# Joining the two products of each scan part on GpSimd ahead of the state-space read-out

## What is computed

```python
def combine(e1, e2):
    a1r, a1i, b1r, b1i = e1
    a2r, a2i, b2r, b2i = e2
    return (a2r * a1r - a2i * a1i, a2r * a1i + a2i * a1r,
            a2r * b1r - a2i * b1i + b2r, a2r * b1i + a2i * b1r + b2i)

_, _, xr, xi = lax.associative_scan(combine, (a_re, a_im, x_re0, x_im0), axis=1)
y = (jnp.einsum('bsgp,ghp->bsgh', xr, c_re.astype(f32))
     - jnp.einsum('bsgp,ghp->bsgh', xi, c_im.astype(f32))
     + d_skip.astype(f32).reshape(SSM_GROUPS, SSM_GROUP) * ug)
y = jax.nn.gelu(y.reshape(bsz, s, SSM_WIDTH)).astype(u.dtype)
```

## Time and profile before

| | us |
|---|---|
| median of three runs | 3403.2 |
| lowest and highest of them | 3398.81 and 3407.45 |
| span of the profiled execution | 3397.2 |
| TensorE busy in it | 3362.4 |
| VectorE busy | 2500.3 |
| ScalarE busy | 1963.3 |
| GpSimd busy | 736.1 |

### The profile page before, as it was taken

The page is one execution under the profiler, slowest core; times in us unless marked ns, Lnnn a source line. Parts: engine busy times, 40 slices in busy tenths (PEclk is TensorE's granted clock), DMA queues, the critical chain, the costliest instruction groups (busy, mean ns, idle before and its releaser), DMA issues.

```text
span 3397.2 us, 80038 instructions
## 1 busy us (share of the span) xinstructions
PE 3362.4 (99%) x29184; PEld 3319.9 (98%) x29184; DVE 2500.3 (74%) x4438; ACT 1963.3 (58%) x3483; POOL 736.1 (22%) x709
## 2 busy tenths in 40 slices
PE   8999999999999999999999999999999999999999
PEld 7999999999999999999999998999999999999999
DVE  7886688788875555676788879998667776666555
ACT  5456655677765555555555556765565665555554
POOL 1001130377777723555000000000000000000000
PEclk9999999999999999999999999999999999999999
DMA  8867788577777766877898864545555555555555
GB/s 325 335 221 253 248 299 303 161 187 190 186 193 194 194 204 225 271 244 249 320 341 338 335 218 132 176 160 183 162 189 192 187 190 192 192 191 196 187 192 179
DMA packets 234085, 758.61 MB, mean 223 GB/s; under 512 B 60072, under 2 KB 63664, under 8 KB 221104
## 3 DMA queue, kind: packets, MB, share of 16 engines
q1 hardware_dynamic: 167328, 608.57, 52.8%
q0 software_dynamic: 62624, 139.63, 15.0%
q10 hardware_dynamic: 3952, 7.91, 0.7%
HBM read 732.78 MB, written 21.11 MB: 222 GB/s over the span
## 4 chain that ended last, share of the span: by engine, by line
PE 94%; DVE 4%; ACT 1%; issue 1%; DMA 1%; DVEq 0%; SPq 0%; ACTq 0%
PE PS L502 24%; PE PS L508 23%; PE PS L507 23%; PE PS L651 7%; PE PS L661 7%; PE PS L659 7%; DVE wlo L1701 1%; DVE big L1695 0%; PE PS L934 0%; DMA raw<-peer_v_dram 0%; PE PS L761 0%; DVE big L1628 0%; PE PS L923 0%; PE PS L880 0%; PE PS L946 0%
## 5 line engine op out<-in xcount | busy, mean ns | idle before, releaser
L1061 ACT ACTIVATE whi<-raw 128x512 fp32r<-128x512 f32 x1864 | 1157.8, 630 | 1022.8 <-PE PS L508 652.3
L1557 DVE TENSOR_TENSOR wlo<-raw,whi 128x512 fp32r<-128x512 f32 x1480 | 1024.9, 706 | 605.9 <-ACT whi L1061 585.6
L502 PE MATMUL PS<-tok_parts_hi,whi 128*128 128x256 f32 x2048 | 569.4, 278 | 0.8 <-ACT big L1286 0.7
L508 PE MATMUL PS<-tok_parts_hi,wlo 128*128 128x256 f32 x2048 | 568.3, 277 | 0.0
L651 PE MATMUL PS<-whi,ev_parts_hi 128*128 128x256 f32 x2032 | 561.8, 276 | 1.1 <-DVE wlo L1557 1.1
L661 PE MATMUL PS<-whi,ev_parts_lo 128*128 128x256 f32 x2032 | 562.1, 277 | 0.0
L507 PE MATMUL PS<-tok_parts_lo,whi 128*128 128x256 f32 x2030 | 561.7, 277 | 0.0
L659 PE MATMUL PS<-wlo,ev_parts_hi 128*128 128x256 f32 x2026 | 559.9, 276 | 0.0
L1701 DVE TENSOR_TENSOR wlo<-raw,whi 128x512 fp32r<-128x512 f32 x564 | 381.6, 695 | 129.2 <-ACT whi L1150 84.1
L434 POOL DMA_INDIRECT gates_dram<-big x256 | 427.0, 1668 | 200.2 <-issue 91.1
L1150 ACT ACTIVATE whi<-raw 128x512 fp32r<-128x512 f32 x436 | 271.4, 629 | 250.4 <-PE PS L508 247.5
(11 more groups left out here) (552 smaller groups left out, 8201.3 us busy)
## 6 DMA issues: line engine op xcount, KB each, us to landing
raw<-peer_u_dram SPq DMA_DIRECT2D x256, 512.0 KB
raw<-peer_v_dram SPq DMA_DIRECT2D x256, 512.0 KB
raw<-w_in_dram SPq DMA_DIRECT2D x240, 512.0 KB
big<-w_mod_dram POOLq DMA_DIRECT2D x96, 1024.0 KB, 6.6
raw<-w_up_dram SPq DMA_DIRECT2D x176, 512.0 KB
raw<-w_down_dram SPq DMA_DIRECT2D x88, 512.0 KB
raw<-w_out_dram SPq DMA_DIRECT2D x64, 512.0 KB
gates_dram<-late POOLq DMA_DIRECT2D x16, 1024.0 KB, 9.0
```

Source lines behind the costliest of these rows:

```text
L502: pe.matmul(out, hi, rhi, start=start, stop=False, **more)
L508: return pe.matmul(out, lo, rhi, start=False, stop=stop, **more)
L1061: f(whi[:, m % PAIRS, quarter(q)], raw[:, m % RING, quarter(q)], ACT.Copy).then_inc(hi_ready, 1)
L1557: dv.tensor_tensor(wlo[:, m % PAIRS, quarter(q)], raw[:, m % RING, quarter(q)], whi[:, m % PAIRS, quarter(q)], ALU.subtract).then_inc(lo_r ...
```

## The change

GpSimd gets two adds for each part, `join(n)`: `ta = ta - tb` when VectorE has finished `tb` (new semaphore `s5_real`), and `p = p + q_` when it has finished `p` (`s5_x`). The read-out then takes two terms, `ta` with `cc[0]` and `p` with `cc[1]`, eight matmuls in place of sixteen, waits for the joins (`s5_joined`), and stands one chunk later (`k == 1`). The negated block of coefficients is no longer made. VectorE waits for `tb` as before, by the new semaphore. The list `RESET` stays.

```diff
--- before.py
+++ after.py
@@ -324,6 +324,7 @@
         lam_in, lam_a, lam_b, lam_c = (sem("l_" + n) for n in "in a b c".split())
         bc_in = [sem(f"s5_bcin{s}") for s in range(2)]
         c_in = sem("s5_cin")
+        s5_real, s5_joined = sem("s5_real"), sem("s5_joined")
         bc_used, s5_lam, s5_raw, s5_bu, s5_angr, s5_sinr, s5_x, s5_y, s5_ys, s5_gel = (
             sem("s5_" + n) for n in "bcused lam raw bu ang sin x y ys gelu".split())
         up_pre, up_silu, act_ready = (sem("up_" + n) for n in "pre silu ready".split())
@@ -473,12 +474,24 @@
                     pool.wait_ge(modw_used, part * KC + kc + 1)
                     pool.dma_start(modring_late[:, kc % MOD_RING, :],
                                    d["w_mod"][part * KC + kc]).then_inc(modw_in[kc % MOD_RING], 16)
+            def join(n):
+
+                p, q_, ta, tb = s5_set[n % 2]
+                pool.wait_ge(s5_real, n + 1)
+                pool.tensor_tensor(ta, ta, tb, ALU.subtract).then_inc(s5_joined, 1)
+                pool.wait_ge(s5_x, n + 1)
+                pool.tensor_tensor(p, p, q_, ALU.add).then_inc(s5_joined, 1)
+
             pool.wait_ge(stage_lo, N_SUB)
             pool.dma_start(cst[:, :, :, :], d["s5_c"]).then_inc(c_in, 16)
             for n in range(8):
                 if n >= 2:
                     pool.wait_ge(bc_used, n - 1)
                 pool.dma_start(bst[:, n % 2, :, :], d["s5_b"][n]).then_inc(bc_in[n % 2], 16)
+                if n >= 2:
+                    join(n - 2)
+            join(6)
+            join(7)
             for r in range(HEADS):
                 pool.wait_ge(qk_ready, 16 + r + 1)
                 if r == 0:
@@ -926,13 +939,13 @@
 
             def read_out(n):
 
-                p, q_, ta, tb = s5_set[n % 2]
-                pe.wait_ge(s5_x, n + 1)
+                p, _, ta, _ = s5_set[n % 2]
+                pe.wait_ge(s5_joined, 2 * n + 2)
                 pe.wait_ge(s5_ys, n)
-                for k, (part, of) in enumerate(((0, ta), (2, tb), (1, q_), (1, p))):
+                for part, of in enumerate((ta, p)):
                     for q in range(4):
                         last = pe.matmul(PS[32 * q:32 * q + 32, 6, 0:SEQ], cc[:, part, 4 * n + q, :], of[:, q, :],
-                                         start=k == 0, stop=k == 3)
+                                         start=part == 0, stop=part == 1)
                 last.then_inc(s5_y, 1)
 
             def spread_two(r):
@@ -988,7 +1001,7 @@
                 if c == 1:
                     mod_turn(3, 7)
                 n, k = divmod(c - SCAN, 5)
-                if k == 0 and 1 <= n <= 8:
+                if k == 1 and 1 <= n <= 8:
                     read_out(n - 1)
                 if k == 3 and -1 <= n < 7:
                     project(n + 1)
@@ -2059,7 +2072,6 @@
                 elif c == 2:
                     link(dv.tensor_tensor(ct[:, 1, :, :], ci, across(cre), ALU.mult))
                 elif c == 3:
-                    dv.tensor_tensor(cc[:, 2, :, :], ct[:, 0, :, :], cc[:, 0, :, :], ALU.subtract)
                     dv.tensor_tensor(cc[:, 0, :, :], cc[:, 0, :, :], ct[:, 0, :, :], ALU.subtract)
                 else:
                     link(dv.scalar_tensor_tensor(cc[:, 1, :, :], cc[:, 1, :, :], -1.0, ct[:, 1, :, :], ALU.mult, ALU.subtract))
@@ -2112,7 +2124,8 @@
                 elif k == 3 and at == 2:
                     dv.tensor_tensor(ta, cos, p, ALU.mult)
                 elif k == 4 and at == 0:
-                    link(dv.tensor_tensor(tb, sin, q_, ALU.mult))
+                    dv.tensor_tensor(tb, sin, q_, ALU.mult).then_inc(s5_real, 1)
+                    dv.wait_ge(s5_real, n + 1)
                 elif k == 4 and at == 1:
                     dv.tensor_tensor(q_, cos, q_, ALU.mult)
                 elif k == 4 and at == 2:
```

## The result

The changed kernel takes **3432.6 us** (median of four runs, 3429.8 to 3438.0); the kernel before, on the same chip, 3401.0 us (3398.0 to 3407.5). The ratio is 1.0092, 95% interval 1.0081 to 1.0104: the change costs about 31 us. The forecast was 3431 us, from 3403.2 us (the median of three of these runs of the kernel before) and 28 us on top.

The account below looks back on a forecast made before the run. TensorE sets the pace, VectorE 3% behind; the joins make VectorE the stage's bound. 24.4 us there plus 3.6 us in the tail give 28 us, on 3403 us: 3431 us, 80% between 3413 and 3446.

Parts of the forecast that it names:

- The bound: Chunks 5 to 44: TensorE sets the pace, VectorE idles only 7.8 us; with the joins VectorE becomes the bound, adding 24.4 us.
- the signs named ahead: Profile after: GpSimd adds of 2.3 us and more, VectorE instructions of 2 to 3 us behind them, TensorE waiting 25 to 35 us.
- One add is one hold: Each 128x1024 GpSimd add locks out VectorE's instructions with two SBUF inputs for its whole length, 2.4 us.
- Who stands behind it: VectorE instructions behind each join: the first join loses 2.4 us, the second 1.85, so 4.25 us a part.
- VectorE's idle time: Chunks 5 to 44: VectorE's 7.8 us of idle time absorb that much of the 32.2 us the joins cost.
- TensorE's saving: Eight matmuls fewer save 0.9 us a read-out, 7 us over eight, hidden once VectorE binds.
- The pace behind it: Dense chunks behind the moved read-outs: eight chunks net slower by 0.3 us each, 2.4 us lost on TensorE.
- The tail: From the last `p` (its end is T) through chunk 46: swap DMAs queued behind `join(7)` delay the rotation, 3.6 us.
- rival C: TensorE's clock falls to 0.50 behind waits the joins make in each part: 13 us more, 3444 us; chance 0.10.
- The landing of the swaps: Tail: the second swap DMA, issued at about T + 3.1, lands 2.2 us later, at T + 5.3.
- A: Rival: GpSimd adds and VectorE hardly block each other, TensorE stays the bound: 3402 us, no change; chance 0.10.
- B: Rival: GpSimd gets in only beside the products from PSUM, costing 1.3 us a join: 15 us, 3418 us; chance 0.13.

Follow-up runs that it names:

- with sixteen matmuls: The changed kernel with each joined term multiplied twice, so its read-outs have sixteen matmuls again: 3432.4 us, 1.0089 to the kernel before.
- the one with fills: The changed kernel with each GpSimd add replaced by a memset of 128x1024 zeros behind the same waits, joins left out of the result: 3401.8 us, 1.001.

## Why the prediction came out right, and where it did not

**The number.** The total is closer than its terms. The change costs 31.5 us where 28 were forecast; the median from which the forecast counted, 3403.2 us, became 3401.0 with the fourth run, and this hides 2.2 of the 3.5 us. That part is luck.

**The bound.** Right. That VectorE stood 7.8 us behind TensorE decided the sign: the joins took some 32 us from it. Of the signs named ahead one did not come as stated: TensorE was to wait 25 to 35 us for `wlo` in the stage, and the list of waits has 11.9. TensorE idled for 17.9 us in all, and the rest of its slack is covered by records that overlap: TensorE's work, 252.15 us before, less the 6.0 us saved, fills 246.1 of the 278.03 us, which leaves 31.9.

**One add is one hold.** Right, and the term of which the trace before showed least. The hold is 2.2 us (forecast 2.4 from 256 columns by a fixed part and a proportional one). Half of the 4497 ns that the Trainium skill ("GPSIMD Engine Reference", section 3.1) has for an add of 2048 elements, an estimate of 2.25 us, is nearer. With a hold of 0.73 us the stage would have grown by 3 us (15 x 0.73 - 7.8), and it grew by 25.5.

**Who stands behind it.** Half right. The first join cost 2.2 us as forecast in kind. For the second I took the middle between 2.4 us and 1.3 us, 1.85; it never reached the products from PSUM, and cost 2.2 as well. The two errors, a smaller hold and a second join at full price, nearly cancel, which is luck: 4.4 us a part against 4.25.

**VectorE's idle time.** All 7.8 us were to be used up; 6.0 were. The stage came to 25.5 us against 24.4.

**TensorE's saving.** 0.86 us a read-out against 0.9. The pace behind it was mis-sized: the later read-out costs 0.5 us of the stage and not 2.4, since the chunks that become faster by it were left out. Neither mattered, both are hidden, as forecast.

**The tail.** The step that failed is "TensorE ... has chunk 46 at the fast pace (5.5 us)". Up to the start of chunk 46 the chain was 0.6 us short (T + 8.0 against T + 8.6; the rotation T + 5.3 against T + 5.7). That is 0.6 us of the 3.4 missing. Then chunk 46 ran for 5.3 us at half clock and took 8.3 us: the other 2.8. The prediction did weigh the clock, as rival C, but only as something in each part. Its own had a stretch of 3.2 us at a clock of 0.50 behind waits of 1.43 and 2.13 us; the forecast's own numbers made TensorE wait from the end of chunk 45 (T + 3.3 before) to T + 8.0, longer than either of these, and the price should at least have been weighed there. That it is always paid does not follow: behind the same two waits in chunks 0 and 1 (1.2 to 1.6 and 2.1 us) the clock fell in ten of the thirteen profiled kernels and stayed at 1.00 in three, with one join, with sixteen matmuls and with the later read-out. The landing of the swaps was forecast at 2.2 us and measured at 2.26 for the second, with some luck: 2.2 is the median of the earlier trace rows, and the 5.0 there belongs to these very swaps, which before landed 4.7 to 5.1 us after issue. The tail came to 7.0 us against 3.6, and 28 forecast became 32.4 in the two windows.

**The rivals.** A, engines that pass each other, falls with `q_` at 3.43 us and with the runs with one join and with none. B, adds only beside products from PSUM, falls too: all sixteen got in behind the split that was running. Placed there by semaphores, as adds of 512 elements, a join costs 0.4 us and not the 1.3 of B. C holds at one place, the tail, and nowhere in the stage, where the granted clock was 1.00 in spite of TensorE's waits of about 1.2 us.

One label in the prediction is off: the stretch of the earlier trace rows holds TensorE's chunks 6 to 45 and the last 2.0 us of chunk 5, not chunks 5 to 44. It is forty chunks either way, and the 7.8 us of idle time are 7.7 in the window used here. And the list of slow chunks lacks chunk 38.

## What to carry to other kernels

Before element work is handed to an idle engine, ask what its instruction takes from the engine that is to be relieved or left alone: here a two-operand add on GpSimd held a nearly full VectorE for 2.2 us, twice what VectorE needs to do it. What was cheap here was an add beside products that read one operand from PSUM (0.2 us lost for 512 elements), and it had to be put there by a semaphore, since by itself it entered behind the split that was running. And a DMA that is due soon must not stand behind a new wait in its queue: the late swaps, and the clock that TensorE lost while it waited for them, cost 7 us at one place, beside the 25.5 us of the stage.

## What was not expected of the hardware

- GpSimd got in at the first boundary between VectorE instructions after its release, 16 times of 16, though VectorE's next instruction was ready. Before the change an add was seen to stand back for three, the one that was running and two splits. What decides this stays open.
- A fill of 128x1024 on GpSimd took 0.96 us and left VectorE's two-operand instructions at their 0.69 and 1.22 us.
- In seven kernels TensorE waited for 2.91 us and more ahead of chunk 46 (2.91 with both joins on VectorE, 3.28, 4.15 twice, 5.40, 6.22 and 6.27), and in all seven it had matmuls at a granted clock of 0.50 behind that wait, for 3.4 us in the first two and 4.5 to 5.8 us in the others. In the first two chunk 46 began at 1.00 and the clock fell 0.4 and 1.2 us later; behind the others the fall came within the wait. After 1.76 us at the same place it stayed at 1.00, as it did in the stage after waits of 1.0 to 1.3 us.
- The same four swap DMAs, issued one directly behind the other, landed 2.2 to 2.6 us after issue in the changed kernel and 4.0 to 4.3 us after it in the one with fills, 1.8 us earlier in the program's course. Before the change they took 4.7 to 5.1 us, some 22 us ahead of T. What makes the difference was not tried; it matters here, since the rotation waits for them.
- Moving the read-out by one chunk costs less than the pace behind a read-out suggests: 0.5 us of the stage, since ten chunks become slower by 2.4 us together and eight others faster by 1.5, with chunk 29 apart.
